# Attention by pairs of heads, with the division by the row sum moved behind the value product

## What is computed

```
def dilated_attention(q, k, v):
    outs, lses = [], []
    for w, d in zip(WINDOWS, DILATIONS):
        o, l = dilated_band_attention(q, k, v, d, w // (2 * d))
        outs.append(o)
        lses.append(l)
    wts = jax.nn.softmax(jnp.stack(lses), axis=0)
    return jnp.sum(wts[..., None] * jnp.stack(outs), axis=0)
```

## Time and profile before

| | us |
|---|---|
| median of 3 runs | 1728.9 |
| lowest, highest | 1719.43, 1733.63 |
| the profiled execution | 1730.85 |
| its span | 1729.0 |
| PE busy in the span | 1607.6 (93%) |
| DVE busy | 892.7 (52%) |
| ACT busy | 610.1 (35%) |
| mean granted clock of TensorE | 0.959 |

### The profile page before, as it was taken

One profiled execution on the slowest core, in us unless ns is written; L12 is line 12 of the kernel. 1 busy time (PEld: TensorE's weight loads), 2 busy tenths in 40 slices (PEclk: granted clock), 3 DMA queues, 4 the chain that ended last, 5 costly groups with the idle time before them and its releaser, 6 DMA issues. The chain is left out here.

```text
span 1729.0 us, 18599 instructions
## 1 busy us (share of the span) xinstructions
PE 1607.6 (93%) x6827; PEld 1192.2 (69%) x6827; DVE 892.7 (52%) x1229; ACT 610.1 (35%) x912; POOL 371.9 (22%) x468
## 2 busy tenths in 40 slices
PE   4899999999999998989989999999989999989967
PEld 3688888887774555333868888888767778766646
DVE  4776337333633442555453333533446545799974
ACT  3322122223433332233343221222433134677644
POOL 3011000000000000000200388820101200399910
PEclk9899999999999999678999999999999999999989
DMA  9688426332231112000423333355223213222201
GB/s 346 208 265 278 158 74 194 97 111 65 82 93 37 37 37 61 0 0 1 106 84 98 98 122 110 98 159 201 61 74 98 78 57 113 74 74 74 85 25 49
DMA packets 203731, 176.34 MB, mean 102 GB/s; under 512 B 6907, under 2 KB 183367, under 8 KB 203142
## 3 DMA queue, kind: packets, MB, share of 16 engines
q1 hardware_dynamic: 188438, 121.87, 23.9%
q0 software_dynamic: 14064, 51.34, 8.4%
q10 hardware_dynamic: 1152, 2.10, 0.3%
HBM read 166.90 MB, written 8.39 MB: 101 GB/s over the span
## 5 line engine op out<-in xcount | busy, mean ns | idle before, releaser
L1939 PE MATMUL ps<-h_hi,w_hi 128*128 128x512 f32 x1224 | 491.5, 402 | 32.3 <-DVE h_lo L1256 17.5
L1941 PE MATMUL ps<-h_hi,w_lo 128*128 128x512 f32 x1224 | 480.7, 393 | 0.0
L1940 PE MATMUL ps<-h_lo,w_hi 128*128 128x512 f32 x1224 | 480.5, 393 | 0.0
L1216 DVE TENSOR_TENSOR w_lo<-w_stage,w_hi 128x1024 fp32r<-128x1024 f32 x225 | 294.7, 1323 | 234.9 <-ACT w_hi L770 232.6
L1939 PEld LDWEIGHTS ps<-h_hi,w_hi 128*128 128x128 f32 x1224 | 232.2, 190 | 108.1 <-issue 55.7
L770 ACT ACTIVATE w_hi<-w_stage 128x1024 fp32r<-128x1024 f32 x225 | 230.8, 1048 | 199.1 <-PE ps L1941 187.7
L1941 PEld LDWEIGHTS ps<-h_hi,w_lo 128*128 128x128 f32 x1224 | 231.9, 189 | 49.9
L1940 PEld LDWEIGHTS ps<-h_lo,w_hi 128*128 128x128 f32 x1224 | 232.2, 190 | 47.0 <-issue 1.2
L1939 PE MATMUL ps<-a_hi,w_hi 128*128 128x512 f32 x544 | 213.8, 393 | 13.1 <-DVE a_lo L1875 9.4
L1940 PE MATMUL ps<-a_lo,w_hi 128*128 128x512 f32 x544 | 212.5, 391 | 0.0
L1941 PE MATMUL ps<-a_hi,w_lo 128*128 128x512 f32 x544 | 212.3, 390 | 0.0
(11 more groups left out here) (416 smaller groups left out, 1635.3 us busy)
## 6 DMA issues: line engine op xcount, KB each, us to landing
w_stage<-in_w_gu SPq DMA_DIRECT2D x88, 512.0 KB, 4.2
ada_w<-in_w_ada POOLq DMA_DIRECT2D x72, 512.0 KB, 5.7
w_stage<-in_w_down SPq DMA_DIRECT2D x44, 512.0 KB, 3.6
w_stage<-in_w_in SPq DMA_DIRECT2D x24, 512.0 KB, 3.8
w_stage<-in_odd_w_in SPq DMA_DIRECT2D x24, 512.0 KB, 3.8
w_stage<-in_even_w_in SPq DMA_DIRECT2D x16, 512.0 KB, 3.9
w_stage<-in_w_out SPq DMA_DIRECT2D x8, 512.0 KB, 3.9
mats<-mats_d POOLq DMA_DIRECT2D x4, 1024.0 KB, 7.4
```

The source lines that it names most:

```text
L1216: dve.tensor_tensor(w_lo[:, c % RING], w_in[:, c % RING], w_hi[:, c % RING].bitcast(F32), ALU.subtract).then_inc(w_split, 1)
L1939: pe.matmul(bank, w_hi[:, slot, k], rhs_hi, start=start, stop=False, skip_group_check=True)
L1940: pe.matmul(bank, w_hi[:, slot, k], rhs_lo, start=False, stop=False, skip_group_check=True)
L1941: return pe.matmul(bank, w_lo[:, slot, k], rhs_hi, start=False, stop=stop, skip_group_check=True)
```

## The change

The steps are renumbered so that two heads alternate: step s is head `s // 8 * 2 + s % 2` and query tile `s % 8 // 2`. In each pair of steps the two score matmuls, one of an even head (partitions 0 to 63) and one of an odd head (64 to 127), are issued one behind the other. The exponentials are no longer multiplied by the reciprocal: `back` waits for ACT's `s_exp` in place of DVE's `p_norm`, and L1536 is gone. The value product is made in every step, with the roles of the operands exchanged: the transposed exponentials (128 by 128) are the stationary operand and the head's 64 value columns stream, which gives rows of the output, queries in partitions. `scale_rows` on DVE multiplies these 128 by 64 values by the reciprocals and puts them into `vt` (at the place of `rope_cos`), and `rows_back` on PE transposes the two heads' 128 by 128 rows into `ps[7]` once in two steps. `pair_hi` and `pair_lo` read `ps[7]`. Two semaphores are merged into one (`edges_zero`) to make room for the new ones; the waits on it keep their places.

```diff
-HI_HEAD, HI_PAIR = [2, 3, 5, 6], [1, 4, 7, 8]
+HI_HEAD, HI_PAIR = [1, 3, 4, 6], [2, 5, 7, 8]
+def head_and_tile(s):
+    return s // 8 * 2 + s % 2, s % 8 // 2
...
             def copy_pt(eng, s):
-                head = s // 4
+                head, tt = head_and_tile(s)
                 eng.wait_ge(pt_t, s + 1)
-                upto(eng, pv_ready, head - 1)
+                upto(eng, pv_ready, s - 7)
...
                     if 1 <= s <= 4 * AH:
                         dve.wait_ge(s_exp, s)
                         link(dve.reciprocal(mx[:, 3, s - 1:s], mx[:, 2, s - 1:s]))
-                        dve.tensor_scalar(e_a[:, (s - 1) % 2], e_a[:, (s - 1) % 2], mx[:, 3, s - 1:s], None, ALU.mult) \
-                            .then_inc(p_norm, 1)
-                    if s >= 2 and s % 2 == 1:
+                    if 3 <= s < 4 * AH + 2 and s % 2 == 1:
                         copy_pt(s - 2)
+                    if s >= 4:
+                        scale_rows(s - 4)
...
+            def scale_rows(s):
+                head, tt = head_and_tile(s)
+                at = slice(head % 2 * DH, (head % 2 + 1) * DH)
+                dve.wait_ge(pv_ready, s + 1)
+                upto(dve, pv_t, 4 * (s // 8 - 1) + tt + 1)
+                dve.tensor_scalar(vt[:, tt, at], ps[6][:, tt * P + at.start:tt * P + at.stop], mx[:, 3, s:s + 1], None,
+                                  ALU.mult).then_inc(pv_scaled, 1)
...
                 def back(s):
-                    pe.wait_ge(p_norm, s + 1)
+                    pe.wait_ge(s_exp, s + 1)
...
-                def values(a_):
-                    off = a_ % 2 * DH
-                    for k in range(2):
-                        pe.wait_ge(pt_ready[k], 2 * a_ + 2)
...
+                def values(s):
+                    head, tt = head_and_tile(s)
+                    pe.wait_ge(pt_ready[s % 2], s // 2 + 1)
...
+                    upto(pe, pv_scaled, s)
                     for st in range(ST):
-                        mm = pe.matmul(ps[6 + a_ // 2 % 2][off:off + DH, :], va[:, st, a_ * DH:(a_ + 1) * DH],
-                                       pt_a[:, a_ % 2, st], start=(st == 0), stop=(st == ST - 1))
+                        mm = pe.matmul(ps[6][:, tt * P + head % 2 * DH:tt * P + (head % 2 + 1) * DH],
+                                       pt_a[:, head % 2, st, tt * P:(tt + 1) * P], va[:, st, head * DH:(head + 1) * DH],
+                                       start=(st == 0), stop=(st == ST - 1))
                     mm.then_inc(pv_ready, 1)
+                def rows_back(s):
+                    tt = head_and_tile(s)[1]
+                    pe.wait_ge(pv_scaled, s + 1)
+                    if tt == 0 and s >= 8:
+                        pe.wait_ge(mix_ready, HI_PAIR[s // 8 - 1])
+                    pe.transpose(ps[7][:, tt * P:(tt + 1) * P], vt[:, tt], ident[:]).then_inc(pv_t, 1)
...
-                for s in range(4 * AH + 3):
+                for s in range(4 * AH + 5):
                     if s == 2:
                         pe.wait_ge(v_done, 8)
-                    if s < 4 * AH:
-                        head, tt = s // 4, s % 4
-                        off = head % 2 * DH
-                        upto(pe, s_max, s - 2)
-                        pe.matmul(ps[s % 3][:], aq[off:off + DH, head // 2, tt * P:(tt + 1) * P],
-                                  ak[off:off + DH, head // 2, :], start=True, stop=True).then_inc(s_ready, 1)
+                    if s < 4 * AH and s % 2 == 0:
+                        upto(pe, s_max, s - 1)
+                        for j in (s, s + 1):
+                            head, tt = head_and_tile(j)
+                            off = head % 2 * DH
+                            pe.matmul(ps[j % 3][:], aq[off:off + DH, head // 2, tt * P:(tt + 1) * P],
+                                      ak[off:off + DH, head // 2, :], start=True, stop=True).then_inc(s_ready, 1)
                     head_part(s)
                     if 2 <= s < 4 * AH + 2:
                         back(s - 2)
-                    if s >= 3 and (s - 3) % 4 == 3:
-                        values((s - 3) // 4)
+                    if 3 <= s < 4 * AH + 3:
+                        values(s - 3)
+                    if s >= 6 and s % 2 == 0:
+                        rows_back(s - 5)
```

More of the change, by code:

```diff
@@ L401, in build_program @@
                                                        sem("mix_hi"), sem("mix_ready"))
-        lnc_in, s_ready, s_max, s_exp, p_norm = sem("lnc_in"), sem("s_ready"), sem("s_max"), sem("s_exp"), sem("p_norm")
+        lnc_in, s_ready, s_max, s_exp = sem("lnc_in"), sem("s_ready"), sem("s_max"), sem("s_exp")
         pt_t, pt_ready, pv_ready = sem("pt_t"), [sem("pt_ready0"), sem("pt_ready1")], sem("pv_ready")
+        pv_scaled, pv_t = sem("pv_scaled"), sem("pv_t")
         s5_in, s5_rows, s5_t, s5_cols = sem("s5_in"), sem("s5_rows"), sem("s5_t"), sem("s5_cols")
@@ L982, in attention @@
                         copy_pt(act, s - 2)
-                    if s >= 3 and (s - 3) % 8 == 7:
-                        pair_hi((s - 3) // 8)
+                    if s >= 13 and (s - 13) % 8 == 0:
+                        pair_hi((s - 13) // 8)
                     head_part(s)
@@ L988, in pair_hi @@
             def pair_hi(i):
-                act.wait_ge(pv_ready, 2 * i + 2)
-                act.activation(a_hi[:, (MH + i) * S:(MH + i + 1) * S], ps[6 + i % 2][:], ACT.Copy).then_inc(mix_hi, 1)
+                act.wait_ge(pv_t, 4 * i + 4)
+                act.activation(a_hi[:, (MH + i) * S:(MH + i + 1) * S], ps[7][:], ACT.Copy).then_inc(mix_hi, 1)
             def copy_pt(eng, s):
-                head = s // 4
+                head, tt = head_and_tile(s)
                 eng.wait_ge(pt_t, s + 1)
-                upto(eng, pv_ready, head - 1)
-                eng.activation(pt_a[:, head % 2, :, (s % 4) * P:(s % 4 + 1) * P],
+                upto(eng, pv_ready, s - 7)
+                eng.activation(pt_a[:, head % 2, :, tt * P:(tt + 1) * P],
                                ps[3][:].rearrange("p (t q) -> p t q", q=P), ACT.Copy).then_inc(pt_ready[0], 1)
@@ L1523, in attention @@
             def attention():
-                for s in range(4 * AH + 2):
+                for s in range(4 * AH + 4):
                     if s < 4 * AH:
@@ L1530, in attention @@
                         upto(dve, s_exp, s - 1)
-                        dve.tensor_tensor_reduce(s_a[:, s % 2], ps[s % 3][:], ln_count[:, s % 4], -1.0, 3e38,
+                        dve.tensor_tensor_reduce(s_a[:, s % 2], ps[s % 3][:], ln_count[:, head_and_tile(s)[1]], -1.0, 3e38,
                                                  ALU.add, ALU.min, mx[:, 0, s:s + 1]).then_inc(s_max, 1)
@@ L1535, in attention @@
                         link(dve.reciprocal(mx[:, 3, s - 1:s], mx[:, 2, s - 1:s]))
[L1536 to L1538 removed]
+                    if 3 <= s < 4 * AH + 2 and s % 2 == 1:
                         copy_pt(s - 2)
[L1540 to L1541 removed]
+                    if s >= 4:
+                        scale_rows(s - 4)
+                    if s >= 14 and (s - 14) % 8 == 0:
+                        pair_lo((s - 14) // 8)
                     denominator(s)
@@ L1548, in pair_lo @@
                 at = slice((MH + i) * S, (MH + i + 1) * S)
-                dve.tensor_tensor(a_lo[:, at], ps[6 + i % 2][:], a_hi[:, at].bitcast(F32), ALU.subtract) \
+                dve.tensor_tensor(a_lo[:, at], ps[7][:], a_hi[:, at].bitcast(F32), ALU.subtract) \
                     .then_inc(mix_ready, 1)
             def copy_pt(s):
-                head = s // 4
+                head, tt = head_and_tile(s)
                 dve.wait_ge(pt_t, s + 1)
-                upto(dve, pv_ready, head - 1)
-                dve.tensor_copy(pt_a[:, head % 2, :, (s % 4) * P:(s % 4 + 1) * P],
+                upto(dve, pv_ready, s - 7)
+                dve.tensor_copy(pt_a[:, head % 2, :, tt * P:(tt + 1) * P],
                                 ps[4][:].rearrange("p (t q) -> p t q", q=P)).then_inc(pt_ready[1], 1)
@@ L1781, in odd_mixer @@
                 dve.wait_ge(cw_ready, 1)
[L1782 removed]
+                dve.wait_ge(edges_zero, 2)
                 def taps(t, third):
```

20 lines of the change are left out of this document (10 added, 10 removed).

## The result

| | before | after |
|---|---|---|
| median (lowest, highest), us | 1727.99 (1719.43, 1733.63) | 1747.3 (1742.42, 1752.58) |
| runs | 4 | 4 |
| ratio of after to before, 95% interval | | 1.0122 [1.0089, 1.0154] |
| the profiled execution, its span | 1730.85, 1729.0 | 1742.42, 1740.6 |
| mean granted clock | 0.959 | 0.951 |

The changed kernel is slower by 19.3 us in the medians. I had forecast 42 us. In the two profiled executions the difference is 11.6 us: the attention takes 14.3 us longer, the scores start 2.6 us earlier, outside of what was changed, and from the projection's first matmul to the end it is 908.3 and 908.2 us.

A forecast was written before the change was run, and what follows sets the result against it. PE was taken to bound the kernel (93% busy). Attention at 1.2 GHz adds 49.8 us, less 7.8 for one fast-clock stretch: 42 us more than 1730.85, so 1773 us profiled, 1771 median; range 1738 to 1795.

The forecast's parts named there:

- the last term of the clock: Attention: one stretch of ten microseconds at 2.4 GHz allowed for, taking 7 to 8 us off the added time.
- The sum at 1.2 GHz: Attention wholly at half clock: two steps 9.96 us, 179.3 us in all, projection starting 49.8 us later.
- The pair: Two neighbouring score matmuls on PE overlap by one record's slot: 2.86 us, not 3.72, at 1.2 GHz.
- The waits: PE's value product waits for DVE's pv_scaled: 1.0 us idle in each of 16 step pairs, nothing in even steps.
- The clock: PE in the attention: 1.2 GHz nearly throughout, since the long full-height value stream that came with all five rises is gone.
- The clock alternates as before: Rival, attention: about half at each clock gives +12 us, 1743 us; range 1738 to 1757, chance 0.20.
- its other case: Within the alternating-clock rival: a third of the attention at 2.4 GHz, 1755 us; the rival's chance is 0.20.
- the sign that I had set for being wrong: Clock column in the profile after showing 1.00 for more than a third of the attention.
- The value product: PE, each step: eight weight loads of exponentials set its price, 1.86 us at 1.2 GHz and 0.95 at 2.4 GHz.
- The clock comes back early and stays: Rival, attention: busy time alone lifts the clock soon after 700 us; 18 us faster, 1713 us, chance 0.15.
- The pair doesn't overlap: Rival, score matmuls on PE: no overlap, 14 us more than the forecast, 1787 us, chance 0.15.
- The wait is hidden: Rival, value product: DVE runs ahead, 16 us go from the sum, 1757 us; no separate chance given.

The follow-up runs named there:

- e3: Changed kernel plus, in odd steps between transposes and value product, an unneeded PE matmul streaming 256 columns (14 in all); 1723.39 us, ratio 0.9982 to the kernel before.
- e5: Changed kernel plus the same 14 unneeded matmuls in the same places, each streaming one column instead of 256; 1745.5 us, ratio 1.0096 to the kernel before.
- e7: Changed kernel with both scaling moves on DVE (ahead of copy_pt, and in even steps of the row maximum) plus 256-column unneeded matmuls; 1702.73 us, ratio 0.9831.
- e6: Changed kernel with scale_rows on DVE ahead of copy_pt and, in even steps, also ahead of the row maximum; 1711.67 us, ratio 0.9877 to the kernel before.
- e2: Changed kernel with the scores issued one per step again, heads still alternating; 1776.53 us, ratio 1.0288 to the kernel before.
- e1: Changed kernel with one swap on DVE, scale_rows ahead of copy_pt; 1715.61 us, ratio 0.9921 to the kernel before.
- e4: Kernel before with only the new step numbering and paired scores, exponentials still normalised before transposing, values still stationary; 1711.02 us, ratio 0.9908.

## Why the prediction was right or wrong

The direction was right, and the size wrong: 42 us were forecast, 19.3 measured. The step that failed is the last term of the clock, "I allow for one such stretch, 7 to 8 us": it measured 29.6 us.

- **The sum at 1.2 GHz** was 179.3 us. PE's busy time, the part at 2.4 GHz doubled, with the idle time as it was, gives 143.8 + 29.6 = 173.4. So the sum was 5.9 us too dear, by two errors that partly cancel. The pair was put at 2.86 us and measured at 1.87 to 2.01: I had read one shared record in the earlier trace rows, where the broadcast starts late for a reason of its own (its first weight load waits 0.95 us for DVE, row below), and took that for the limit of the overlap. In 16 pairs this is some 15 us. The waits were put at 16 × 1.0 and measured at 24.9 in all: 1.12 to 1.14 in odd steps, as forecast, but 0.23 at 1.2 GHz to 0.69 at 2.4 GHz in the even steps without mLSTM work, where I had nothing, and 0.85 to 1.15 in front of three broadcasts, which wait for ACT. The weight load of that broadcast in the kernel before:

```profile
704.18 0.50 PEld L2063 LDWEIGHTS ps<-rs,ident 36*128 36x128 f32 x2 [0.95 <-DVE num_f L1503]
```

- **The clock** failed. Of the attention 44.4 us ran at 2.4 GHz, where I allowed ten. In them PE was busy 29.6 us, which is what they gave back, against my 7.8. In the prediction's own terms: 44.0 us longer at the half clock throughout (173.4 − 129.4, forecast 49.8), less 29.6 us that the fast clock gave back (forecast 7.8), is the 14.3 us by which the attention grew (rounded). The rival "The clock alternates as before", at a chance of 0.20, was what happened. That the profiled execution took 1742.42 us, just its 1743, is in part luck: that price was for half of the attention at each clock, and measured were 31% at 2.4 GHz, nearest to its other case, a third and 1755 us. Nor did the sign that I had set for being wrong, the fast clock for more than a third of the attention, appear; it was set too far out, since 31% was already worth 29.6 us.
- **Why it failed.** From five rises that all came with the long value product I concluded that without it there would be hardly any. Those rows show what came with a rise, not that nothing else does. The trace of the kernel before had a counterexample at its start, which I overlooked: from 20.27 us PE does nothing but 128 by 128 transposes, one in 0.21 us, and at 24.3 us, still among them, the pace shows the clock's rise: from there they come every 0.11 us (PE's groups of instructions from 21 to 24 us and from 24.5 to 25.6 us, with busy us, and the mean length of one in ns):

```profile
L1910 PE MATMUL ps<-ident,x_rows 128*128 128x128 f32 x16 | 3.6, 421 | 0.0
L1910 PE MATMUL ps<-ident,x_rows 128*128 128x128 f32 x12 | 1.5, 272 | 0.0
```

  The end of the program, where I saw the clock fall at once, isn't evidence either: between the last one-column matmul and the fall of the clock PE stood for 1.32 us (in front of its last transposes at 1720.51). In the changed kernel the clock rises seven times in the attention, twice of them after a sum of squares and transposes (rows of its timeline of PE; the clock rises at 718.4):

```profile
715.03 2.07 PE L2192 MATMUL ps<-sq,ones 128*128 128x512 f32 x2
716.90 1.06 PE L2156 MATMUL ps<-ident,e_a 128*128 128x128 f32 x4
```

- I had named the sums of squares and priced them once. The other rise after one is at 759.3; the five at 691.1, 732.0, 773.0, 800.3 and 827.6 follow on transposes, value products and scores, two of them (732.0, 773.0) with a broadcast among these.
- **What was right.** The direction, and its reason: the exchange saves PE nothing, and more of the attention runs at 1.2 GHz (69% against 49%). "What it changes is what PE does in that time": e3 against e5 shows it, and e7 against e6 points the same way. The value product was put at 1.86 and 0.95 us and measured at 1.60 to 1.86 and 0.86 to 1.01; `scale_rows` at 0.25 and measured at 0.28; and the granted clock stayed at 1.2 GHz through 20.4 us with PE busy for 18.13, and through 23.7 us with PE busy for 21.00, against the rival "The clock comes back early and stays" (1713). "The pair doesn't overlap" (1787) is refuted by e2, "The wait is hidden" (1757) by the wait itself.
- **What I didn't see** is that the two costs are coupled. I priced the wait at 16 us; taking most of it away gave 32, because the stretches at 1.2 GHz shortened with it. In e1 the half clock costs 30.0 us, no more than in the kernel before (31.7). So the 12.9 us of clock that the changed kernel lost came with the gaps and the new mix together: close the gaps (e1) or add streaming (e3), and they are gone. In e6, with still fewer gaps, the cost was 35.2 in its one profile, so the two don't separate cleanly. What in PE's work makes the clock rise stays open beyond this: no run tells at which mix of loads, streams and gaps it turns.

The spread of the runs is the clock too. The four runs of the changed kernel took 1742.42, 1744.84, 1749.76 and 1752.58 us at mean clocks of 0.951, 0.949, 0.945 and 0.944; the fastest run of e7 (1693.45) had 0.974, its slowest (1714.71) 0.960. The profiled execution of the changed kernel was its fastest, so its profile shows less of the loss than the median does.

## What to carry to other kernels

When a change exchanges the operands of a matmul, count its PE time and then ask what the clock will do with the new mix: here the same busy time, with more loading, shorter streams and gaps of a microsecond, cost some 13 us by the clock alone. Where a new step closes a loop between two engines, look at what stands ahead of it in the other engine's list: a swap of two lines turned a loss of 1.2% into a gain of 0.8%. A change that is slower as a whole can hold a part that is a gain; run the parts alone before it is dropped (the pairs alone give 0.9%).

## What the runs showed of the hardware that I had not expected

- Two float32 matmuls of 64 rows, on the two halves of the array, take the time of one: four records in 1.06 us at 2.4 GHz and in 1.87 to 2.01 us at 1.2 GHz. Not one slot of four is saved, but two.
- Fourteen useless matmuls of 256 columns made the program 24 us faster (1747.3 to 1723.39); the same ones with one column did nothing (1745.5).
- Much of e6's attention ran at the half clock at a PE busy share of 94% (mean clock 0.69), while the full clock was granted for more of the time at 77% (e4, 85.66 of 111.00 us busy, 0.87).
- Where the gaps are closed, what is left of PE's idle time sits in the stretches at 2.4 GHz: in e1 0.4 of 10.8 us and in e7 none of 6.7 us fell into the half clock. In the changed kernel, where PE waits in every odd step, it was 10.2 of 24.9 us. DVE keeps its pace when PE slows down: its copy takes 0.69 us at 1.2 GHz (699.63) as at 2.4 GHz.
